# Hybrid encoder step on one core: the fourth weight sum of a gate/up pair moves from VectorE to GpSimd

## The reference

```python
h = _rmsnorm(x, norm_mix)
mix, hg_s = _hgrn2(h, ...)          # 8 heads of 128: gated linear recurrence
x = x + mix
gate, up = jnp.split(_rmsnorm(x, norm_ffn) @ w_gu, 2, axis=-1)   # 1024 x (2 * 2816)
x = x + (jax.nn.silu(gate) * up) @ w_down                        # 2816 x 1024
```

## Time and profile before

| | |
|---|---|
| runs | 2657.01 us median of 3 (2654.47 to 2660.84) |
| the profiled execution | 2656.22 us, of which the span from first to last instruction is 2654.5 us |
| busy in the span | PE 98%, DVE 68%, ACT 48%, POOL 10% |
| granted TensorE clock, mean | 0.994 |
| gate/up stages of block 0 | 372 to 432 us, 472 to 567 us and 617 to 717 us, roughly |

### The profile page before, as it was taken

How to read it: one execution, slowest core, us unless ns; L and a number is a source line. 1 busy time by engine, 2 the same in 40 slices (tenths; PEclk the granted TensorE clock), 3 DMA queues, 4 the chain that set the end, 5 groups by cost and what they waited for, 6 DMA issues and landing times.

```text
span 2654.5 us, 53882 instructions
## 1 busy us (share of the span) xinstructions
PE 2594.3 (98%) x16804; PEld 2372.7 (89%) x16804; DVE 1801.2 (68%) x3183; ACT 1275.4 (48%) x2315; POOL 277.4 (10%) x197
## 2 busy tenths in 40 slices
PE   8999989999999998999999999999999999999998
PEld 7999989999988887998988888899998888799897
DVE  6666687868756677765656676766665676766565
ACT  5545554434445556443435555534344555644343
POOL 4111110000021112000011111100002111200001
PEclk9999999999999999999999999999999999999999
DMA  5321345645542224775653222667554222467574
GB/s 185 94 63 59 116 156 178 206 149 192 163 138 68 71 75 128 213 215 166 214 152 92 68 78 83 209 183 223 159 179 140 71 75 71 140 204 219 162 220 145
DMA packets 203414, 379.70 MB, mean 143 GB/s; under 512 B 23168, under 2 KB 23200, under 8 KB 203056
## 3 DMA queue, kind: packets, MB, share of 16 engines
q1 hardware_dynamic: 202896, 369.73, 45.0%
q0 software_dynamic: 384, 8.44, 0.9%
HBM read 331.67 MB, written 52.74 MB: 145 GB/s over the span
## 4 chain that ended last, share of the span: by engine, by line
PE 87%; DVE 6%; issue 4%; ACT 2%; DMA 1%; POOL 0%; SPq 0%; DVEq 0%; ACTq 0%; POOLq 0%
PE ps L437 16%; PE ps L439 15%; PE ps L438 15%; PE ps L529 9%; PE ps L530 9%; PE ps L531 9%; PE ps_s L529 2%; PE ps_s L531 2%; PE ps_s L530 1%; PE ps_u L340 1%; PE ps_s L319 1%; PE ps_o L353 1%; PE ps_u L341 1%; PE ps_o L355 1%; PE ps_o L354 1%
## 5 line engine op out<-in xcount | busy, mean ns | idle before, releaser
L529 PE MATMUL ps<-h,g_hi 128*128 128x256 f32 (+1 forms) x2112 | 609.1, 288 | 28.1 <-DVE ebuf L1208 9.5
L531 PE MATMUL ps<-h,g_lo 128*128 128x256 f32 (+1 forms) x2112 | 605.2, 287 | 0.0
L530 PE MATMUL ps<-h,g_hi 128*128 128x256 f32 (+1 forms) x2112 | 604.9, 286 | 0.0
L925 DVE TENSOR_TENSOR w_lo<-w_raw,w_hi 128x512 fp32r<-128x512 f32 x512 | 372.6, 730 | 238.8 <-ACT w_hi L745 238.7
L437 PE MATMUL ps<-h_hi,w_hi 128*128 128x512 f32 (+1 forms) x1280 | 472.6, 369 | 14.9 <-DVE h_lo L930 9.2
L745 ACT ACTIVATE w_hi<-w_raw 128x512 fp32r<-128x512 f32 x512 | 318.0, 625 | 326.2 <-PE ps L439 310.3
L439 PE MATMUL ps<-h_hi,w_lo 128*128 128x512 f32 (+1 forms) x1280 | 452.8, 354 | 0.0
L438 PE MATMUL ps<-h_lo,w_hi 128*128 128x512 f32 (+1 forms) x1280 | 451.0, 352 | 0.0
L529 PEld LDWEIGHTS ps<-h,g_hi 128*128 128x128 f32 x2112 | 402.2, 190 | 38.3 <-DVE ebuf L1208 15.8
L437 PE MATMUL ps<-a_hi,w_hi 128*128 128x512 f32 (+1 forms) x1200 | 429.1, 358 | 7.4 <-DVE w_lo L925 4.5
L438 PE MATMUL ps<-a_lo,w_hi 128*128 128x512 f32 (+1 forms) x1200 | 422.6, 352 | 0.0
(11 more groups left out here) (169 smaller groups left out, 3784.4 us busy)
## 6 DMA issues: line engine op xcount, KB each, us to landing
w_raw<-w_all SPq DMA_DIRECT2D x516, 256.0 KB, 2.6
g_raw<-w_all SPq DMA_DIRECT2D x286, 256.0 KB, 3.5
g_x<-kept_sum SPq DMA_DIRECT2D x132, 256.0 KB, 3.5
g_hi<-kept_hi SPq DMA_DIRECT2D x132, 256.0 KB, 2.8
g_lo<-kept_lo SPq DMA_DIRECT2D x132, 256.0 KB, 3.1
kept_sum<-g_x SPq DMA_DIRECT2D x44, 256.0 KB, 3.1
kept_hi<-g_hi SPq DMA_DIRECT2D x44, 256.0 KB, 2.5
kept_lo<-g_lo SPq DMA_DIRECT2D x44, 256.0 KB, 2.7
```

What stands on the lines that cost most here:

```text
L529: pe.matmul(out, g_hi[:, o, k, :].bitcast(F32R), hh, start=(k == 0 and not more), stop=False, skip_group_check=True)
L530: pe.matmul(out, g_hi[:, o, k, :].bitcast(F32R), hl, start=False, stop=False, skip_group_check=True)
L531: mm = pe.matmul(out, g_lo[:, o, k, :].bitcast(F32R), hh, start=False, stop=last, skip_group_check=True)
L925: nc.vector.tensor_tensor(w_lo[:, r, :, :], w_raw[:, r, :, :], w_hi[:, r, :, :].bitcast(F32), ALU.subtract).then_inc(w_lo_ready, 1)
```

## The change

In block 0 the sum S4 is taken out of VectorE's queue and put into GpSimd's, where a loop over all 22 pairs stands between two `sum_squares`. It waits for A12, for the low part of S2 and for the count 3 of `g_sum_ready`. Since two engines now raise `g_sum_ready`, VectorE's sums get two new waits so that the counts stay in order: S1 waits for the fourth sum of the pair before, S3 for the end of S2.

```diff
                 if o == S1:
                     dve.wait_ge(g_loaded[RAW_A21], 16 * (j + 1))
                     dve.wait_ge(g_loaded[RAW_A22], 16 * (j + 1))
+                    wait(dve, g_sum_ready, 4 * j)
                     wait(dve, g_lo_ready, OPERANDS * j)
...
-                elif o == S3:
+                else:
+                    dve.wait_ge(g_sum_ready, 4 * j + 2)
                     wait(dve, g_sum_stored[0], 16 * j)
                     nc.vector.tensor_tensor(g_x[:, 2], g_raw[:, RAW_A11], g_raw[:, RAW_A21], ALU.subtract).then_inc(g_sum_ready, 1)
-                else:
-                    dve.wait_ge(g_loaded[RAW_A12], 16 * (j + 1))
-                    dve.wait_ge(g_lo_ready, OPERANDS * j + S2 + 1)
-                    dve.wait_ge(g_sum_ready, 4 * j + 3)
-                    nc.vector.tensor_tensor(g_x[:, 1], g_raw[:, RAW_A12], g_x[:, 1], ALU.subtract).then_inc(g_sum_ready, 1)
...
                 low(S3, S1)
-                total(S4)
...
-                        if first(b) and m == A12:
-                            weight_sum(j1, S4)
...
-                    if first(b) and i == 3:
-                        weight_sum(0, S4)
...
         def _(pool):
+            def fourth_sum(j):
+                pool.wait_ge(g_loaded[RAW_A12], 16 * (j + 1))
+                pool.wait_ge(g_lo_ready, OPERANDS * j + S2 + 1)
+                pool.wait_ge(g_sum_ready, 4 * j + 3)
+                nc.gpsimd.tensor_tensor(g_x[:, 1], g_raw[:, RAW_A12], g_x[:, 1], ALU.subtract).then_inc(g_sum_ready, 1)
+
...
-                sum_squares(2 * b + 1, T)
+                if first(b):
+                    sum_squares(2 * b + 1, T)
+                    with pool.Fori(0, FT) as j:
+                        fourth_sum(j)
+                else:
+                    sum_squares(2 * b + 1, T)
                 sum_squares(2 * b + 2, TB)
```

## The result

| | before | after |
|---|---|---|
| median of 16 runs, us | 2658.67 (2654.47 to 2662.87) | 2665.11 (2661.36 to 2668.57) |
| ratio after to before, compared on the same chips | | 1.0019, 95% interval 1.0012 to 1.0026 |
| profiled execution: span, us | 2654.5 | 2663.4 |
| PE, DVE, POOL busy us | 2594.3, 1801.2, 277.4 | 2595.8, 1805.6, 312.0 |

The kernel is slower by 0.19% (0.12 to 0.26), some 5 us (3.2 to 6.9); forecast were +2.9 us and a measured time of 2659.9, range 2653 to 2668. The interval leaves out zero, and it leaves out the +2.9 by a little; by the line of 0.2% that the prediction drew, the result counts as the same, to which it gave 0.59. VectorE has 22 additions less (3161 instructions for 3183), and is yet busy for 4.4 us more.

A forecast was written before the change was run, and what follows sets the result against it. In 16 block 0 pairs a loop through VectorE's L1208 and TensorE's S4 was taken as the bound. Steady pairs 2.3, second pairs 0.8, first pairs 0.4, pair 0 −0.6 gave +2.9 us: 2657.0 + 2.9 = 2659.9, range 2653 to 2668.

The forecast's parts named there:

- The loop through L1208: Block 0's gate/up pairs: TensorE's S4 waits for L1208 in 16 pairs, so VectorE's chain time there is span time.
- At most 0.44 us a pair could be gained: Wait before S4 in block 0: shortening VectorE's chain gains only up to TensorE's recorded idle 0.44 us.
- The port: Shared SBUF read port in a steady pair: GpSimd's sum ends 1.15 us after `a_low`, costing VectorE 0.74 us.
- The wait at S3: VectorE's S3 waits for S2's end: 0.11 us later, 0.07 absorbed before `a_low`, leaving +0.04 us.
- A steady pair: Each of 13 steady pairs in block 0 loses 0.18 us: 0.74 and 0.04 less 0.60; 2.3 us in all.
- First pairs of groups 1 and 2: No `a_low` there: L1208 starts 0.5 us late, 0.3 us is slack, so 0.2 us each, 0.4 us together.
- Pair 0: Without L1152 the low part of A22 is done sooner, TensorE resumes earlier: −0.6 us, port cost hidden in the normalisation wait.
- the side effect that the prediction left with an open sign: TensorE's half clock from 360 to 370 us might end sooner or not, shifting a microsecond or two either way.
- the one that the port costs nothing: Rival: VectorE keeps the port to S1's low part, GpSimd works under L1208; −8 us, 2649; chance 0.12.
- the one with GpSimd ahead of `a_low`: Rival: GpSimd gets the port first or takes longer; up to 0.54 us more in 18 pairs, +13 us, 2670; chance 0.13.
- the first rival: The offload works: GpSimd's sum runs under L1208, 16 pairs give 7.5 us, −8 with pair 0, 2649; chance 0.12.
- The rival by which nothing shows: ScalarE or VectorE's idle 0.36 us takes up part of the delay in a pair; 2657; chance 0.05.

The follow-up runs named there:

- e1_narrow: The changed kernel with GpSimd's fourth sum covering one column instead of 512, all waits kept; ratio 0.9974, −6.9 us against the kernel before.
- e8_moved2: The kernel before with the fourth sum still on VectorE, moved between the low parts of A22 and A12, pair 0 as before; ratio 0.9969, −8.2 us.
- e9_extra2: The kernel before plus an extra GpSimd product of two different 128x512 tiles in 21 pairs, released by S2's low part; ratio 1.0052, +13.8 us.
- e2_waits: The kernel before with only the two new waits among the sums, fourth sum still on VectorE; ratio 1.0005, +1.3 us.
- e10_own: The changed kernel with the fourth sum counted on its own semaphore, so without the two new VectorE waits; ratio 1.0011, +2.9 us against the kernel before.
- e7_not0: The changed kernel with pair 0's fourth sum back on VectorE; ratio 1.0013, +3.5 us against the kernel before.
- e11_both: e8_moved2 with pair 0's fourth sum also moved behind the low part of A22; ratio 0.9966, −9.0 us against the kernel before.
- e5_extra: The kernel before plus an extra GpSimd subtraction of a 128x512 tile from itself in 21 pairs, released by S2's low part; ratio 1.0031, +8.2 us.
- e6_only0: The changed kernel with only pair 0's fourth sum on GpSimd, the others back on VectorE, new waits kept; ratio 0.9998, −0.5 us against the kernel before.
- e3_late: The changed kernel with GpSimd's fourth sum waiting for S1's low part instead of S2's; ratio 0.9985, −4.0 us against the kernel before.

## Why the prediction came out as it did

- **The loop through L1208 sets the pace.** Right. Taking 0.6 us out of it (e1_narrow) or moving 0.6 us behind it (e8_moved2) gives 7 to 8 us; adding 0.73 us to it (e9_extra2) costs 0.73 in each pair.
- **At most 0.44 us a pair could be gained.** Too low, and it changed nothing in the forecast of the loss. The pace fell by 0.59 us in e1_narrow and 0.62 in e8_moved2. The idle time in a row isn't the price of a wait. TensorE ahead of and behind the waiting pass of the earlier trace rows, kernel before:

```profile
407.57 0.29 PE L531 MATMUL ps<-h,g_lo 128*128 128x288 f32 x1
...
408.54 0.29 PE L530 MATMUL ps<-h,g_hi 128*128 128x288 f32 x1
```

  Passes with nothing in their way start 0.13 us apart and overlap, each being recorded as 0.29 or 0.30 long; idle time is counted from the recorded end of the last one. The waiting pass started 0.73 us behind the one ahead (407.57 to 408.30), which is 0.60 more than 0.13, and the next 0.24 us behind it, 0.11 more. So a wait recorded as 0.44 us costs 0.6 to 0.7. The pace of 11.88 less 0.71 is 11.17, which is what the first pairs of groups 1 and 2 take with no wait (11.16).
- **The port: 0.74 us a pair.** Right, 0.75 in the changed kernel's rows, 0.73 alone in e9_extra2. GpSimd ends 1.16 us behind `a_low` (forecast 1.15). The row of block 1 with the same order of operations was the right one to take.
- **The wait at S3: +0.11, 0.07 of it absorbed.** Right: 0.12 and 0.07, worth 0.02 and 0.03 in the pace of e2_waits and of e10_own.
- **A steady pair loses 0.18 us.** Right, 12.04 for 11.87 us.
- **First pairs of groups 1 and 2: 0.2 us each.** Mis-sized. They lost 0.44 us (11.60 for 11.16 between the copies of bank A). VectorE there, kernel after:

```profile
478.71 0.68 DVE L1153 TENSOR_TENSOR g_lo<-g_x,g_hi 128x512 fp32r<-128x512 f32 x1
479.31 0.45 DVE L1197 TENSOR_TENSOR ebuf<-ps,ebuf 128x288 f32<-128x288 f32 x1
479.68 2.32 DVE L1153 TENSOR_TENSOR g_lo<-g_x,g_hi 128x512 fp32r<-128x512 f32 x2
481.93 0.74 DVE L1204 TENSOR_TENSOR ebuf<-ps,ebuf 128x576 f32<-128x576 f32 x1
```

  From the low part of S2 to L1204 it is 3.22 us, where it was 2.78: 0.44 us, and S3's 0.12 ahead of it makes L1204 0.56 us late, about the forecast 0.5. The error is in what TensorE makes of it. TensorE there, with the passes ahead of S4's first and behind it:

```profile
482.32 0.29 PE L531 MATMUL ps<-h,g_lo 128*128 128x288 f32 x1
...
483.03 0.29 PE L530 MATMUL ps<-h,g_hi 128*128 128x288 f32 x1
```

  A pass that waits for L1208 starts 0.05 us behind its end, so of the 0.33 us between 480.82 and 481.15 only 0.28 was slack. After, S4 starts 0.15 us behind L1204's end (482.67 to 482.82), 0.10 more than that, and its second pass 0.21 us behind the first instead of 0.13. Counted from the copy of bank A, 0.56 − 0.28 + 0.10 + 0.08 is 0.46, beside the 0.44 measured: the slack did count, and the start of a pass that had to wait cost 0.18 that the forecast had at nothing. The same sum gives e10_own's 0.24 us, where L1204's counterpart is 0.35 us late. Why the first pass starts 0.15 us behind here, and 0.05 in steady pairs, isn't settled.
- **What the sum left out.** The load of A22 has little reserve. In the changed kernel two pairs (12.32 and 12.53 us long, 0.3 and 0.5 over the pace) have S1 standing 0.2 and 0.4 us for it. VectorE before S1 in the second of these, kernel after:

```profile
645.38 0.69 DVE L1153 TENSOR_TENSOR g_lo<-g_raw,g_hi 128x512 fp32r<-128x512 f32 x1 [0.30 <-ACT g_hi L805]
646.49 0.69 DVE L1140 TENSOR_TENSOR g_x<-g_raw 128x512 f32<-128x512 f32 x1 [0.42 <-DVE g_lo L1153]
```

  The releaser named is VectorE's own earlier result, long done; the load of A22 is the other thing that S1 waits for, and was issued at 642.37. That the change makes these two loads late isn't shown. In the profiles of e1_narrow, e7_not0, e8_moved2, e10_own and e11_both one or two pairs have such a wait too; the kernel before, e2_waits, e5_extra, e6_only0 and e9_extra2 have none.
- **Pair 0: −0.6 us.** The cause was right and the gain wasn't kept. TensorE resumed after 4.21 us instead of 4.82, and ScalarE copied bank A of pair 0 0.9 us sooner, counted from TensorE's stop. It then stood for 3.47 us before S4. The profile names a low part as what ended this, but S4 also waits for L1204 and started 0.11 us behind its end. VectorE ahead of it, kernel after, and S4's first pass in the kernel before:

```profile
367.47 2.30 DVE L1153 TENSOR_TENSOR g_lo<-g_x,g_hi 128x512 fp32r<-128x512 f32 x2
369.69 0.74 DVE L1204 TENSOR_TENSOR ebuf<-ps,spare 128x576 f32<-128x576 f32 x1
```

```profile
371.73 0.37 PE L529 MATMUL ps<-h,g_hi 128*128 128x288 f32 x1 [0.62 <-issue]
```

  The two low parts took 1.29 us before: this is the port again, 1.0 us of it, under pair 1's fourth sum (GpSimd, 367.36 to 368.63). The prediction let pair 0's port cost fall into the wait for the normalisation. Only L1209 waits for that (0.44 us, 370.88); S4 doesn't, and L1204 stands in its way. In e1_narrow, with the same order and the low parts at 1.28 us, TensorE stood for 2.56 us. Even so S4 began 0.5 us sooner than before, counted from the stop (15.7 us for 16.2). From S4 to the copy of bank A in pair 1 it is then 6.1 us (370.54 to 376.63), where it was 4.7 (371.73 to 376.40). The granted clock, kernel after, in three windows, and behind them the last window of the kernel before:

```profile
359.00:363.00 4.00, 3.43 (x15) 3.12 (x15) 2.34 (x2) 1.56 (x3) 1.10 (x1) 0.57 0.65 181
363.00:369.00 6.00, 4.07 (x28) 3.50 (x26) 5.45 (x8) 3.36 (x5) 1.27 (x1) 1.00 0.27 73
370.00:376.00 6.00, 5.46 (x23) 5.49 (x24) 3.55 (x6) 3.75 (x7) 0.00 (x0) 0.50 0.86 279
...
370.00:376.00 6.00, 5.38 (x36) 4.65 (x36) 4.44 (x8) 5.91 (x10) 0.52 (x1) 1.00 0.68 252
```

  It came back to 1.00 (2.4 GHz) for 363 to 369 us, TensorE ran through its products at that level, idled, and worked on at 0.50 (1.2 GHz) from 370 to 376, where the kernel before had 1.00. TensorE's passes start 0.24 us apart there instead of 0.13. So the side effect that the prediction left with an open sign took some 1.4 us here, and pair 0 came out 0.9 us longer instead of 0.6 shorter. It goes both ways: e9_extra2 stood for 3.59 us at this place, and its passes behind that started 0.13 us apart, as at the upper level.

In the trace, pairs 1 to 21 lost 4.5 us (323.9 to 328.4): 13 × 0.16 = 2.1 in steady pairs, 3 × 0.25 = 0.8 in second ones, 2 × 0.44 = 0.9 in first ones, and the rest, 0.8, at A22's load. With pair 0's 0.9 (less than the spread of pair 0 among the kernels that leave it alone, 20.4 to 22.7 us) that is 5.4 us, beside the 5.0 measured. The steps of the prediction that were off are thus in the last addition: the first pairs and pair 0 were 0.5 and 1.5 us too good, and the load was missing. That the total fell into the forecast (0 to +8 us) owes something to luck: what these terms left out is about as large as the forecast loss itself, and all of it went the same way. The profiled executions differ by 8.9 us; the 3.5 us outside block 0's gate/up stages aren't accounted for by the change, and the runs of either kernel differ by 7 to 8 us among themselves.

Of the rivals, the one that the port costs nothing fell by the rows (GpSimd was held 0.4 us and the low parts 0.75), and so did the one with GpSimd ahead of `a_low`: in every pair of the trace that has an `a_low`, it came 0.24 us too late for that. What the first rival would have given, −7 to −8 us, is what e1_narrow shows. The rival by which nothing shows fell with the pace of 12.04 us and an interval that leaves out zero.

## What to carry to other kernels

An addition moved from VectorE to GpSimd isn't off VectorE's path as long as VectorE reads two SBUF tiles at that moment: here it took 0.75 us from VectorE to save 0.60. And read a wait's price off the starts of the instructions, not off the idle time recorded: 0.44 us of idle time was worth 0.6 to 0.7 here. Look for the instruction behind which the critical engine is released (L1208) and put the work behind that one, on whichever engine: one place later for GpSimd's release gave −4 us and, better, the sum left on VectorE three instructions later gave −8. Then check what stands behind the new place; one instruction decided between −2 and −8 us, since ScalarE's silu was queued behind a result that had become late.

## What the runs showed of the hardware that was not expected

A GpSimd subtraction of 128x512 whose two inputs are the same tile took 1.04 us, with two different tiles 1.28 us. The Trainium skill (SBUF — State Buffer, section Who interferes with whom) says that who blocks is decided by the order of issue; the runs agree and put a size to it: with VectorE's instruction first, GpSimd stood 0.4 us and VectorE's next SBUF reader 0.75 us (e5_extra, with the shorter instruction, about 0.5 us), and with GpSimd first, under a PSUM reader, GpSimd stood not at all and VectorE 0.6 us (e3_late).
